# A step between the recurrence's loads and its first mix, masked keys one step earlier, and fewer side slots beside the gated products, in a hybrid encoder layer

## What is computed

```python
h = sandwich_ffn(x, ffn1...)                        # x + 0.5*rms(swiglu(rms(x)))
z = rms_norm(h, mix_pre_g) @ w_in
z_q, z_k, z_v, z_rw, z_g = split(z)
o_att = diff_attention(z_q, z_k, z_v, ...)          # 4 heads, two softmax maps
o_rw  = rwkv7_branch(z_rw, S0, shift0, p)           # 8 heads of 64, a state of 64x64 each
merged = gate_att * (o_att @ w_o_att) + gate_rw * (o_rw @ w_o_rwkv)
h = h + rms_norm(merged @ w_out, mix_post_g)
y = sandwich_ffn(h, ffn2...)
```

```python
prev = concatenate([shift0, z_rw[:, :-1]]);  zs = z_rw + (prev - z_rw) * rwkv_mu
S = S * w_t + sa * (kk_t * a_t) + v_t * k_t;  y_t = S @ r_t
```

## Time and profile before

| what | value |
|---|---|
| median of 3 executions | 3051.14 us (3048.3 to 3056.46) |
| the profiled execution's own time | 3051.44 us |
| its span, first to last instruction | 3049.6 us |
| TensorE matmul busy | 2957.0 us, 97% of the span |
| VectorE busy | 1731.7 us, 57% |
| ScalarE busy | 1359.4 us, 45% |
| GpSimd busy | 397.8 us, 13% |
| mean granted TensorE clock | 0.99 |
| DMA moved | 500.44 MB, mean 164 GB/s |

### The profile page before, as it was taken

How to read it: one execution, slowest core, us unless ns; L and a number is a source line. 1 busy time by engine, 2 the same in 40 slices (tenths; PEclk the granted TensorE clock), 3 DMA queues, 4 the chain that set the end, 5 groups by cost and what they waited for, 6 DMA issues and landing times.

```text
span 3049.6 us, 59679 instructions
## 1 busy us (share of the span) xinstructions
PE 2957.0 (97%) x24182; PEld 2622.9 (86%) x24182; DVE 1731.7 (57%) x3061; ACT 1359.4 (45%) x2748; POOL 397.8 (13%) x738
## 2 busy tenths in 40 slices
PE   8999999999999899999999999999999999999997
PEld 8999988887878778988888788887888989899997
DVE  5445543644574464574775655746756846656454
ACT  4335444532444333543544445444545444554333
POOL 1001001211321210210211101201112100010000
PEclk9999999999999999999999999999999999999999
DMA  5445556754664565653655643535655424665443
GB/s 168 128 128 166 166 163 211 234 161 124 211 200 153 177 196 158 208 157 93 216 184 163 208 156 117 184 93 174 193 171 168 139 86 156 200 212 167 126 128 121
DMA packets 504465, 500.44 MB, mean 164 GB/s; under 512 B 29096, under 2 KB 402112, under 8 KB 504176
## 3 DMA queue, kind: packets, MB, share of 16 engines
q1 hardware_dynamic: 475968, 406.36, 42.7%
q0 software_dynamic: 28224, 90.26, 9.5%
HBM read 443.03 MB, written 54.47 MB: 163 GB/s over the span
## 4 chain that ended last, share of the span: by engine, by line
PE 90%; DVE 5%; issue 2%; ACT 2%; DMA 1%; POOL 1%; SPq 0%; ACTq 0%; DVEq 0%; POOLq 0%
PE ps L280 44%; PE ps L290 30%; PE ps L1095 2%; PE ps L1105 1%; PE ps L1897 1%; PE ps L1878 1%; PE ps L302 1%; PE ps L1812 1%; DVE wlo L244 1%; PE ps L1087 1%; PE ps L1111 1%; PE ps L1823 1%; PE ps L1236 1%; PE ps L1849 1%; PE ps L1889 1%
## 5 line engine op out<-in xcount | busy, mean ns | idle before, releaser
L244 DVE TENSOR_TENSOR wlo<-raw,whi 128x512 fp32r<-128x512 f32 x1140 | 784.0, 690 | 794.4 <-ACT whi L236 791.5
L236 ACT ACTIVATE whi<-raw 128x512 fp32r<-128x512 f32 x1140 | 712.8, 628 | 589.4 <-PE ps L280 344.8
L280 PE MATMUL ps<-xnhi,whi 128*128 128x384 f32 x2688 | 927.3, 345 | 5.9 <-DVE xnlo L557 5.9
L280 PE MATMUL ps<-xnhi,wlo 128*128 128x384 f32 x2688 | 902.5, 336 | 0.0
L280 PE MATMUL ps<-xnlo,whi 128*128 128x384 f32 x2688 | 901.9, 336 | 0.0
L280 PEld LDWEIGHTS ps<-xnhi,whi 128*128 128x128 f32 x2688 | 507.3, 189 | 31.2 <-issue 15.6
L280 PEld LDWEIGHTS ps<-xnlo,whi 128*128 128x128 f32 x2688 | 507.3, 189 | 2.5 <-issue 1.9
L280 PEld LDWEIGHTS ps<-xnhi,wlo 128*128 128x128 f32 x2688 | 506.5, 188 | 0.0
L290 PE MATMUL ps<-whi,hidhi 128*128 128x512 f32 x936 | 384.0, 410 | 20.4 <-DVE xnlo L557 12.4
L290 PE MATMUL ps<-whi,hidlo 128*128 128x512 f32 x936 | 369.0, 394 | 0.0
L290 PE MATMUL ps<-wlo,hidhi 128*128 128x512 f32 x936 | 368.5, 394 | 0.0
(11 more groups left out here) (323 smaller groups left out, 3326.2 us busy)
## 6 DMA issues: line engine op xcount, KB each, us to landing
raw<-in_ffn_w_in_dram SPq DMA_DIRECT2D x528, 256.0 KB, 3.0
raw<-in_ffn_w_out_dram SPq DMA_DIRECT2D x264, 256.0 KB, 2.7
raw<-in_w_in_dram SPq DMA_DIRECT2D x252, 256.0 KB, 3.0
xt<-h_scratch SPq DMA_DIRECT2D x42, 512.0 KB, 6.2
att<-in_cache_att_k_dram POOLq DMA_DIRECT2D x64, 256.0 KB, 4.7
att<-in_cache_att_v_dram POOLq DMA_DIRECT2D x64, 256.0 KB, 3.4
rw<-zr_scratch POOLq DMA_DIRECT2D x51, 256.0 KB, 7.3
raw<-in_w_out_dram SPq DMA_DIRECT2D x48, 256.0 KB, 2.9
```

The source lines that it names most:

```text
L236: act.activation(B["whi"][:, slot], B["raw"][:, slot], ACT.Copy).then_inc(E["whi"], 1)
L244: dve.tensor_tensor(B["wlo"][:, slot], B["raw"][:, slot], B["whi"][:, slot].bitcast(F32), ALU.subtract).then_inc(E["wlo"], 1)
L280: ins = pe.matmul(ps[:, bank, 0:BT], B["w" + wt][:, n % RING, i * P:(i + 1) * P], x(xt, i), start=first and i == 0 and (wt, xt) == passes[ ...
```

## The change

It has three parts. First, a step LW is put between LD and ML. On VectorE the wait for the low-rank inputs and their mix move from LD to LW, and LD is empty there; GpSimd's loads stay in LD. LD and LW together cost 3.5 in the planner where LD cost 3. Second, masked keys: VectorE masks the keys of step 0 at the end of YY, and those of step q+1 in the middle of NS number q, after TensorE's second signal of that step; a step NS now costs 1.5 and not 1. Third, the room of the first 17 slabs of OP goes from 0.6 to 0.45.

```diff
-        "yt uzk y bk bk ns nsd ns nsd bk bk ns nsd ns nsd bk bk ns nsd ns nsd bk bk ns nsd ns nsd", "yc var yn"),
+        "yt uzk y bk bk ns nsd bk bk ns nsd ns nsd bk bk ns nsd ns nsd bk bk ns nsd ns nsd ns nsd", "yc var yn"),
...
         lora = slot(S_L)
+        yield "LD"
         dve.wait_ge(E["rw_ld_l"], 48 * (p + 1))
...
         dve.tensor_tensor(lora[:, 0:256], lora[:, 0:256], lora[:, 256:512], ALU.add).then_inc(E["rw_zl"], 1)
-        yield "LD"
+        yield "LW"
...
+            def masked(q):
+                for i, src in enumerate((S_BT, S_KT)):
+                    dve.tensor_scalar(slot(S_BK[i]), slot(src), B["rc"][:, 16 + q:17 + q], None, ALU.mult).then_inc(E["rw_kept_v"], 1)
+
+            masked(0)
             yield "YY"
             for q in range(4):
-                if q:
-                    dve.wait_ge(*done(E, "nsp", 2 * q))
-                else:
-                    dve.wait_ge(*done(E, "yz", 1))
-                for i, src in enumerate((S_BT, S_KT)):
-                    dve.tensor_scalar(slot(S_BK[i]), slot(src), B["rc"][:, 16 + q:17 + q], None, ALU.mult).then_inc(E["rw_kept_v"], 1)
                 for s in TWO:
+                    if s and q < 3:
+                        dve.wait_ge(*done(E, "nsp", 2 * q + 2))
+                        masked(q + 1)
...
-RW_COST = {"O": 1.5, "LD": 3, "ML": 2, "L": 1.5,
+RW_COST = {"O": 1.5, "LD": 1.5, "LW": 2, "ML": 2, "NS": 1.5, "L": 1.5,
...
-                room[s] = 0.6
+                room[s] = 0.45
```

More of the change, by code:

```diff
@@ L2347, in late_pool @@
     yield
-RW_COST = {"O": 1.5, "LD": 3, "ML": 2, "L": 1.5, "WA": 1.5, "G": 1.5, "CX": 1.5, "PD": 1.5, "P1": 1.5, "P2": 1.5, "P3": 1.5, "P4": 1.5, "C2": 1.5, "C3": 1.5, "C4": 1.5, "ST": 2.5}
+RW_COST = {"O": 1.5, "LD": 1.5, "LW": 2, "ML": 2, "NS": 1.5, "L": 1.5, "WA": 1.5, "G": 1.5, "CX": 1.5, "PD": 1.5, "P1": 1.5, "P2": 1.5, "P3": 1.5, "P4": 1.5, "C2": 1.5, "C3": 1.5, "C4": 1.5, "ST": 2.5}
 ATT_COST = {"LD0": 4, "LD": 2, "T": 1.5}
@@ L2355, in rw_steps @@
 def rw_steps(p):
-    names = ["LD", "ML", "L", "WA", "G", "CX", "PD", "P1", "P2", "P3", "P4", "FA", "FK", "MAB", "QA", "QK", "S2", "S4", "X1", "X2", "X3", "HH", "R1", "R2", "R3", "VA0", "VA1"]
+    names = ["LD", "LW", "ML", "L", "WA", "G", "CX", "PD", "P1", "P2", "P3", "P4", "FA", "FK", "MAB", "QA", "QK", "S2", "S4", "X1", "X2", "X3", "HH", "R1", "R2", "R3", "VA0", "VA1"]
     names += ["US", "SS"] * 2 if p else ["ST"] * 2 + ["UT", "UZ", "YY"] + ["NS"] * 4 + ["BK"] * 4
```

## The result

The changed kernel takes **3033.2 us** (median of 4 executions, 3031.3 to 3034.0), the kernel before 3051.7 on the same chip. The ratio is 0.9939, with a 95% interval of 0.9926 to 0.9952: 18.5 us faster where 29.5 were forecast. The direction was right and the time lies in the range, but over a third of the gain is missing. The profiled execution took 3033.4 us.

What follows compares the result with a forecast made beforehand. TensorE, busy 2957.0 of 3049.6 us, bounds the kernel; only its waits and half clock can be had. 22.5 + 5.2 + 4.8 - 1 - 2 = 29.5 us less than 3051.4 gives 3022 us, bounds 3010 to 3031, range 3010 to 3042.

Steps and rivals of the forecast that it cites:

- The new step between loads and mix: Pairs 1, 2 and 7: waits for low-rank inputs and the half clock behind them go, 8.5, 6.4 and 7.6, together 22.5 us.
- the step of 47%: Behind VectorE's waits in pairs 1, 2 and 7, half clock loses 47% of what TensorE works in the stretch.
- at least 6.1 us: Lead of loads over mix: three slabs of 2.04 us without side work; in pair 1 nothing taken as left of 7.50.
- Masked keys: Pair 0: keys made a step ahead end TensorE's three waits; gain 5.2 us, bounds 3 and 5.2.
- Room beside gated products: First output projection: FA moves from slab 571 to 570; gain 4.8 us with half clock, bounds 0 and 10.2.
- Now FA's three operations, 0.68 us each, stand ahead: VectorE at FA, slab 570: they run from 1552.6 to 1554.6, so ScalarE's copy is done at 1554.5.
- 7.5 becomes 4.1: TensorE's wait at FA: 2.3 us left there plus 1.8 for the later maximum's exponentials; 3.4 us gained before half clock.
- The bound of 0: Lower bound of the 4.8 us gain from FA's move: the wait only changes its name.
- P1 beside V1: Pair 1, P1 from slab 345 to 347: its GpSimd operations delay two cached-value loads; cost 1 us, bounds 0 and 1.7.
- New meetings: Moved steps elsewhere meeting a busy VectorE: cost 2 us, bounds -3 and 19; as a rival 3052 us, chance 0.08.
- late loads: Rival: loads get a third less DMA share, waits return in pairs 1 and 7, some 10 us lost; 3032 us, chance 0.13.
- Weights did not run dry: Rival denied here: weight loads land too late in each of nine pairs, 57 us slower; 3079 us, chance 0.05.

Runs made afterwards that it cites:

- experiment 3: The kernel before with step LW, loads three slabs ahead of the mix and masked keys a step ahead, other steps in old slabs: 3030.3 us, 0.9924.
- experiment 4: The kernel of experiment 3 with pair 1's first mix at slab 331 not 330, ML at 333, L at 335: 3024.0 us, 0.9917 to the kernel before.
- experiment 5: The changed kernel with step P1 of pair 1 at slab 346 and not 347: 3031.6 us, 0.9934 to the kernel before.
- experiment 7: The kernel of experiment 3 with only FA of pair 4 moved, to slab 570 from 571: 3028.2 us, 0.9922 to the kernel before.
- experiments 1: The kernel before with only step LW and loads three slabs ahead of the mix, other steps in old slabs: 3036.0 us, 0.9948.
- 8: The changed kernel with the steps of slabs 576 to 616 back at the kernel before's slabs, FA still at 570: 3031.9 us, 0.9935.
- 10: The kernel of experiment 4 with pair 4's steps moved later, no recurrence step between slabs 563 and 573: 3020.5 us, 0.9897 to the kernel before.

## Why the prediction was partly right

**The new step between loads and mix: right.** 22.5 us forecast, 21.7 measured in the change (9.0, 7.4, 5.3), 22.7 in experiment 3 before what pair 1 gave back, and 22.3 in experiment 4, which gave nothing back there. Half clock went with the waits, as the step of 47% said, though experiment 5's execution, with the same slabs there, has 3.4 us of it again behind pair 7. What the text put into three slabs was too tight, though: it held "at least 6.1 us" against the 7.50 us that VectorE had waited, and the chain is 9.0 us from the first issue, 13.5 to r. It did not show since the planner had set the mix 11.1 us and ML 19.6 us behind. Pair 7 got 5.3 of 7.6, since line 604 still waits 1.6 us there.

**Masked keys: right**, 5.2 us forecast, 5.4 measured alone. The 7.4 us of the changed kernel's slabs 260 to 320 hold a change of the clock besides, of the kind that the last section shows, and steps moved by one slab.

**Room beside gated products: wrong**, 4.8 us of gain forecast, a loss of 2.5 measured. The step that failed is "Now FA's three operations, 0.68 us each, stand ahead", from which "7.5 becomes 4.1" was taken. It followed one chain, maximum, exponentials, copy, and gave the time between to TensorE. VectorE had been busy for 27.1 of 27.5 us up to that point, which the trace of before shows. At slab 573 TensorE now does not wait at all, but FA one slab earlier met P4's copy on that queue (2.8 us), and what TensorE gained by arriving earlier it waited at the gated products of slab 580 (3.8 us). The bound of 0, "the wait only changes its name", was the outcome of FA alone. That the gain did not come is shown by experiment 7 and the tables after it; that the stretch became slower by 2.5 us is not clear of its variation, 2.0 us.

**P1 beside V1: size wrong, cause open.** The term of 1 us, bounds 0 to 1.7, was 5.1. It counted the delay on GpSimd alone. The longer operation took 2.08 us and not 1.68, TensorE's wait grew from 1.4 to 2.2 us, and the larger part is half clock: 6.8 us at 877, at 47% 3.2 us, and 3.4 us at 860, 1.6 us, ahead of P1's operations. The text had given each wait of VectorE's a second price of this kind and left it out here. Since experiment 4 pays nearly the same with P1 in its old slab, it stays open how much of the 5.1 us is P1's.

**New meetings: 2 us forecast, 2.0 measured** over all other slabs, a sum of many single gains and losses of 1 to 3 us. That the two agree is luck. So is the time's place in the range: its upper part was put in for late loads with some meetings, and the time came to lie there by the two terms above, each outside its own bounds. **The rivals:** late loads did occur in experiments 1 and 3, by distance and not by share of the DMA engines; in the change VectorE still waits for them 1.32 us in pair 2 and 3.3 us in pair 0. Weights did not run dry: ScalarE waits 14.6 us in all for `raw`, 17.5 us before.

## What to carry to other kernels

When a wait is priced by one chain, first ask whether the engine at its end had any pause ahead of it: with a busy share near 1 over the stretch another order may only rename the wait, as it did here in every table tried. A moved load needs its distance in time from the first issue to the last landing that each user needs, here 9.0 and 13.5 us, in slabs of that place. Where a short wait is added to TensorE, its half clock may cost more than the wait (here 3.2 us behind 2.2). And a gain or loss of 2 or 3 us in one stretch of one trace is to be believed when it repeats in another.

## What the runs showed of the hardware

GpSimd's power in P1 (`ALU.pow` on 128x8 values) took 2.08 us in the changed kernel and in experiments 5 and 8, and 1.68 us in the kernel before; the maximum ahead of it, of the same size, took 0.45 us in the changed kernel and 0.60 us before. So neither has one fixed price in these traces.

The granted clock of one stretch of the same program differs between executions. The kernels of 3, 4 and 10 are the same up to slab 326. For 702 to 720 us, where pair 0's state steps lie, they show (same columns as above, in this order):

```profile
702.00:720.00 18.00, 18.00 (x308) 16.38 (x308) 5.21 (x9) 2.54 (x6) 0.00 (x0) 0.81 0.12 34
```

```profile
702.00:720.00 18.00, 18.00 (x276) 16.87 (x274) 3.75 (x6) 1.48 (x3) 0.00 (x0) 0.62 0.11 31
```

```profile
702.00:720.00 18.00, 18.00 (x291) 16.45 (x290) 4.92 (x13) 1.89 (x6) 0.00 (x0) 0.72 0.13 39
```

A step of 0.09 to 0.10 over 18 us is 1.6 to 1.8 us at full clock, with no edit ahead of it that would explain it. The kernel of 4 ran from 3021.8 to 3033.4 us, so differences of a few us between two kernels are hard to tell from medians.
